# Two transformer blocks with eight experts: experts sorted by token count, three of them with a stacked high and low left operand

## The reference

```python
def moe_swiglu(h, w_router, w_gate, w_up, w_down):
    logits = jnp.einsum('bsd,de->bse', h.astype(F32), w_router.astype(F32))
    top_val, top_idx = lax.top_k(logits, TOP_K_EXPERTS)          # 2 of 8
    top_w = jax.nn.softmax(top_val, axis=-1)
    combine = jnp.sum(jax.nn.one_hot(top_idx, N_EXPERTS, dtype=F32) * top_w[..., None], axis=-2)
    for e in range(N_EXPERTS):
        out = out + combine[..., e:e + 1] * swiglu(h, w_gate[e], w_up[e], w_down[e])   # 1024 -> 2816 -> 1024
```

## Time and profile before

| | |
|---|---|
| median of 3 runs | 1914.62 us (1911.88 to 1915.4) |
| profiled execution, span | 1912.1 us |
| TensorE busy | 1824.1 us, 95% |
| VectorE busy | 1416.6 us, 74% |
| ScalarE busy | 1122.6 us, 59% |
| GpSimd busy | 392.8 us, 21% |
| mean granted TensorE clock | 0.983 |
| DMA | 506.45 MB, mean 265 GB/s |

### The profile page before, as it was taken

One profiled execution on the slowest core, in us unless ns is written; L12 is line 12 of the kernel. 1 busy time (PEld: TensorE's weight loads), 2 busy tenths in 40 slices (PEclk: granted clock), 3 DMA queues, 4 the chain that ended last, 5 costly groups with the idle time before them and its releaser, 6 DMA issues.

```text
span 1912.1 us, 26024 instructions
## 1 busy us (share of the span) xinstructions
PE 1824.1 (95%) x8799; PEld 1486.2 (78%) x8799; DVE 1416.6 (74%) x1631; ACT 1122.6 (59%) x1296; POOL 392.8 (21%) x315
## 2 busy tenths in 40 slices
PE   7899999989999998899989879999999999999997
PEld 6678886868888786688878667888888888888885
DVE  5748874466976586644458758889888888888897
ACT  6745444564443464443345537777777777777775
POOL 3722203463212363200046500000000000000000
PEclk9999999999999999999999989999999999999999
DMA  8348884418987341455544258999999999999994
GB/s 271 111 161 327 343 342 147 149 54 323 344 347 275 91 152 45 154 195 179 192 154 142 69 187 334 386 376 386 380 384 376 383 383 381 380 374 381 381 387 167
DMA packets 237934, 506.45 MB, mean 265 GB/s; under 512 B 23304, under 2 KB 74720, under 8 KB 231712
## 3 DMA queue, kind: packets, MB, share of 16 engines
q1 hardware_dynamic: 225664, 492.91, 70.9%
q0 software_dynamic: 3008, 10.32, 2.0%
q10 hardware_dynamic: 9184, 2.23, 0.5%
HBM read 497.49 MB, written 7.91 MB: 264 GB/s over the span
## 4 chain that ended last, share of the span: by engine, by line
PE 83%; DVE 7%; issue 6%; ACT 3%; POOL 1%; DMA 0%; POOLq 0%; SPq 0%; DVEq 0%; ACTq 0%
PE bank L2351 25%; PE bank L2353 25%; PE bank L2352 25%; PE bank L2470 2%; ACT slab L2042 1%; PE bank L2789 1%; DVE slab L1290 1%; PE bank L2561 1%; PE bank L2539 1%; ACT w_hi L1892 1%; PE bank L2521 1%; POOL w_lo L826 1%; DVE x L1074 0%; PE bank L2572 0%; DVE slab L1271 0%
## 5 line engine op out<-in xcount | busy, mean ns | idle before, releaser
L977 DVE TENSOR_TENSOR w_lo<-slab,w_hi 128x2048 fp32r<-128x2048 f32 x369 | 847.8, 2308 | 214.3 <-ACT w_hi L1892 213.3
L1892 ACT ACTIVATE w_hi<-slab 128x2048 fp32r<-128x2048 f32 (+2 forms) x421 | 796.6, 1898 | 329.0 <-PE bank L2353 256.3
L2351 PE MATMUL bank<-w_hi,hT_hi 128*128 128x512 f32 (+3 forms) x1664 | 649.4, 390 | 14.2 <-DVE hT_lo L1012 4.4
L2352 PE MATMUL bank<-w_lo,hT_hi 128*128 128x512 f32 (+3 forms) x1664 | 638.0, 383 | 0.0
L2353 PE MATMUL bank<-w_hi,hT_lo 128*128 128x512 f32 (+3 forms) x1664 | 637.9, 383 | 0.0
L2351 PEld LDWEIGHTS bank<-w_hi,hT_hi 128*128 128x128 f32 x1664 | 316.0, 190 | 77.9 <-DVE w_lo L977 8.8
L2353 PEld LDWEIGHTS bank<-w_hi,hT_lo 128*128 128x128 f32 x1664 | 315.5, 190 | 59.7
L2352 PEld LDWEIGHTS bank<-w_lo,hT_hi 128*128 128x128 f32 x1664 | 316.3, 190 | 55.3
L826 POOL TENSOR_TENSOR w_lo<-slab,w_hi 128x512 fp32r<-128x512 f32 (+2 forms) x208 | 262.4, 1295 | 381.3 <-ACT w_hi L1892 361.6
L2351 PE MATMUL bank<-w_hi,hid_hi 128*128 128x512 f32 x680 | 265.6, 391 | 0.7 <-DVE w_lo L977 0.7
L2353 PE MATMUL bank<-w_hi,hid_lo 128*128 128x512 f32 x680 | 265.0, 390 | 0.0
(11 more groups left out here) (252 smaller groups left out, 1232.0 us busy)
## 6 DMA issues: line engine op xcount, KB each, us to landing
slab<-in_w_exp_gate SPq DMA_DIRECT2D x176, 512.0 KB, 7.0
slab<-in_w_exp_up SPq DMA_DIRECT2D x176, 512.0 KB, 7.5
slab<-in_w_exp_down SPq DMA_DIRECT2D x176, 512.0 KB, 7.1
slab<-in_w_ada SPq DMA_DIRECT2D x48, 1024.0 KB, 5.5
slab<-in_w_mlp_in SPq DMA_DIRECT2D x64, 512.0 KB, 5.4
slab<-in_w_mlp_out SPq DMA_DIRECT2D x64, 512.0 KB, 9.0
slab<-in_w_in SPq DMA_DIRECT2D x56, 512.0 KB, 5.0
slab<-in_w_out SPq DMA_DIRECT2D x32, 512.0 KB, 4.6
```

The costliest lines, as they stand in the source:

```text
L977: dve.tensor_tensor(w_lo[:, q, 0:n], raw(s)[:, 0:n], w_hi[:, q, 0:n].bitcast(F32), ALU.subtract).then_inc(lo_dve, 1)
L1892: act.activation(w_hi[:, q, 0:n], raw(s)[:, 0:n], ACT.Copy).then_inc(hi_done, 1)
L2351: pe.matmul(dst, a_hi, b_hi, start=start, stop=False)
L2352: pe.matmul(dst, a_hi, b_lo, start=False, stop=False)
```

## The change

The inner columns of an expert are cut into three blocks of 768, 1024 and 1024 (`E_WIDTH`), each accumulated in two banks for gate and two for up. Weight tiles of gate and up hold two k blocks of a whole inner block, so a row of them is 3 or 4 KB long in HBM, where it was 2 KB (1 KB for the step of 256). An expert has 36 tiles (`MT`), eight of 1536 and two of 1024 columns among them, where it had 33. The sequence of a body is up, gate, the down tiles of the block before, turn. Down tiles of the last block run in the next body, with all three products.

The experts but number 0 are sorted on VectorE by the number of their tokens (`sort`, inside the first body): the four with the most take bodies 1, 3, 5 and 7, the others 2, 4 and 6 (`order`, read by SyncE for the addresses). In bodies 2, 4 and 6 the list has 64 places (`SHORT`). Its stationary operand is 128 columns wide all the same: columns 0 to 63 are the high parts, 64 to 127 the low parts, so that two products, with `w_hi` and with `w_lo`, give what three gave, plus low x low; the two halves of the result are added later: ScalarE moves rows 64 to 127 to rows 0 to 63 of SBUF, VectorE adds them, for gate and up. The output keeps both halves, and GpSimd adds them to `y_rows` by two scatters in turn. A second round follows if a list in a short body has more than 64, or another more than 128 entries. The residuals of all tiles are written by VectorE in one operation each.

The core of the diff:

```diff
-F_WIDE = 512
+
+E_WIDTH = (768, 1024, 1024)
+E_FROM = (0, 768, 1792)
+MS = len(E_WIDTH)
+MT = 36
+SHORT = P // 2
+SHORT_AT = (2, 4, 6)
+ROUND_SUMS = 16 * (3 + 4 + 2 * 3)
 ...
+        def is_short(p, first):
+
+            return p == 0 and not first
 ...
+        def up_tile(j, first):
+
+            return (0 if first else -4, 8, 20)[j]
+
+        def gate_tile(j, first):
+
+            return (4 if first else 0, 12, 24)[j]
+
+        def down_tile(j):
+
+            return (4, 16, 28, MT - 4)[j + 1]
+
+        def tile_width(r, first, last):
+
+            if r in (18, 19):
+                return D
+            return 2 * E_WIDTH[0] if r < 4 or first and r < 8 or r >= MT - 4 and not last else TILE
 ...
+                        def wide_rows(w, j, n, r0):
+
+                            for b in range(4):
+                                to, loaded = slot_free(n, r0 + b)
+                                d = to[:, 0:2 * E_WIDTH[j]].rearrange("p (k n) -> p k n", k=2)
+                                for k in range(2):
+                                    sp.dma_start(d[:, k:k + 1, :], w[:, 2 * b + k:2 * b + k + 1, E_FROM[j]:E_FROM[j] + E_WIDTH[j]]
+                                                 ).then_inc(loaded, 16)
 ...
+                            if n == n0 + 1:
+                                sp.wait_ge(order_done, 1)
+                            wg, wu, wd = weights(0 if first else sp.value_load(order[0:1, n - n0:n - n0 + 1], min_val=0, max_val=NE - 1))
+                            wide_rows(wu, 0, n, up_tile(0, first))
 ...
+                for a, o in enumerate((slice(0, SHORT), slice(SHORT, P)) if at in SHORT_AT else (slice(0, P),)):
+                    pool.wait_ge(scattered, done - (16 if at not in SHORT_AT else 32) + 16 * a)
+                    pool.indirect_dma_start(y_rows, bass.IndirectOffsetOnAxis(index[n % 2][0:o.stop - o.start, 0:1], 0), y_out[o, :], None,
+                                            compute_op=ALU.add).then_inc(scattered, 16)
 ...
+                    mark(dve.tensor_copy(rank_at[:, 0:1], iota[:, 0:1]))
+                    mark(dve.tensor_copy(rank_at[:, 1:NE:2], iota[:, 1:1 + NE // 2]))
+                    mark(dve.tensor_copy(rank_at[:, 2:NE:2], iota[:, 1 + NE // 2:NE]))
+                    mark(dve.memset(spare, 0.0))
+                    mark(dve.tensor_copy(counts[:, 1:NE], tot[:, 0, 1:NE]))
+                    link(dve.memset(counts[:, 0:1], 2.0 * SEQ))
+                    link(dve.memset(spare[:, 2:NE:2], float(P - SHORT)))
+                    mark(dve.tensor_tensor(at, across(counts), down_(counts), ALU.is_gt))
+                    link(dve.tensor_tensor(same, across(counts), down_(counts), ALU.is_equal))
 ...
+                    for src, to in ((wts, ranked_wts), (pos, ranked_pos)):
+                        link(dve.tensor_tensor(picked, each, src.unsqueeze(2).broadcast_to([P, TT, NE, NE]), ALU.mult))
+                        link(dve.tensor_reduce(to, picked, AX.X, ALU.add))
+                    link(dve.tensor_tensor(same, at, across(iota[:, 0:NE]), ALU.mult))
+                    link(dve.tensor_reduce(turns, same, AX.X, ALU.add))
+                    dve.tensor_copy(order[:, :], turns[0:1, :]).then_inc(order_done, 1)
 ...
+                    link(dve.tensor_tensor(counts, counts, spare, ALU.add))
+                    link(dve.tensor_reduce(den[0:1, 0, 0:1], counts[0:1, :], AX.X, ALU.max))
+                    dve.tensor_copy(flag[0:1, 0:1], den[0:1, 0, 0:1]).then_inc(flag_done, 1)
 ...
+                        def activated(j):
+
+                            at = ub + n * (2 * MS) + 2 * j
+                            banks = (bank[6], bank[7]) if first and j == 1 else (bank[4], bank[5])
+                            w = half_of(j)
+                            if short:
+                                base = half_base(turn_, i, j)
+                                for c, o in enumerate(halves(j)):
+                                    dve.wait_ge(half_moved, base + c + 1)
+                                    dve.tensor_tensor(mact[0:SHORT, o], bank[c][0:SHORT, 0:w], mact[0:SHORT, o], ALU.add
+                                                      ).then_inc(half_added, 1)
+                                for c, o in enumerate(halves(j)):
+                                    dve.wait_ge(half_moved, base + c + 3)
+                                    dve.tensor_tensor(up_low[:, o], banks[c][0:SHORT, 0:w], up_low[:, o], ALU.add
+                                                      ).then_inc(half_added, 1)
+                                for c, o in enumerate(halves(j)):
+                                    dve.wait_ge(act_done, at + c + 1)
+                                    dve.wait_ge(half_added, base + c + 3)
+                                    dve.tensor_tensor(mact2[0:SHORT, o], mact[0:SHORT, o], up_low[:, o], ALU.mult).then_inc(sq_done, 1)
+                            else:
+                                for c, o in enumerate(halves(j)):
+                                    dve.wait_ge(act_done, at + c + 1)
+                                    dve.tensor_tensor(mact2[:, o], mact[:, o], banks[c][:, 0:w], ALU.mult).then_inc(sq_done, 1)
 ...
+                        lows(2 if first else -2, gate_tile(0, first) + 6)
+                        activated(0)
+                        if first:
+                            lows(10, 14)
+                        else:
+                            lows(6, 10)
+                        hidden_low(0)
+                        if short:
+                            dve.wait_ge(w_used, FREE_SPLIT + EXPERT0 + n * MT + 8)
+                            dve.tensor_scalar(hid_lo[:, :, :], ones[:, 0:1].unsqueeze(2).broadcast_to([P, 4, SEQ]), 0.0, None, ALU.mult
+                                              ).then_inc(hid_zero, 1)
+                        if first:
+                            dve.nop().then_inc(hid_zero, 1)
+                        if first and n0 == 0:
+                            sort()
+                        if not last:
+                            lists(ranked_pos, ranked_wts, SHORT if p == 1 else P, 2 * i + p + 1, n + 1)
+                        lows(14 if first else 10, 18)
+                        activated(1)
 ...
+                            make_index(1 - p, n + 1, bank[6], None if first else sums_after(turn_, i, 0) if p else sums_after(turn_, i, 0) - 32)
+                            lows(22, 30)
 ...
+                            listed_rows(1 - p, n + 1, p == 1)
+                            lows(30, 34)
+                            hidden_low(2)
 ...
+                                    base = half_base(turn_, i, j)
+                                    for c, o in enumerate(halves(j)):
+                                        act.activation(mact[0:SHORT, o], bank[c][SHORT:P, 0:w], ACT.Copy).then_inc(half_moved, 1)
+                                    for c, o in enumerate(halves(j)):
+                                        act.activation(up_low[:, o], banks[c][SHORT:P, 0:w], ACT.Copy).then_inc(half_moved, 1)
+                                    for c, o in enumerate(halves(j)):
+                                        act.wait_ge(half_added, base + c + 1)
+                                        act.activation(mact[0:SHORT, o], mact[0:SHORT, o], ACT.Silu).then_inc(act_done, 1)
 ...
+                        def both(dst, hi_, lo_, q, s, start, stop_):
+
+                            if lo_ is None:
+                                pe.matmul(dst, hi_, w_hi[:, q, s], start=start, stop=False)
+                                return pe.matmul(dst, hi_, w_lo[:, q, s], start=False, stop=stop_)
+                            return product(dst, hi_, lo_, w_hi[:, q, s], w_lo[:, q, s], start, stop_)
+
+                        def rows_by(dst, j, r0):
+
+                            w = half_of(j)
+                            for b in range(4):
+                                q = low_ready(r0 + b)
+                                for k in (2 * b, 2 * b + 1):
+                                    l_hi, l_lo = lhs_listed(k + KC * p, 0)
+                                    for c in range(2):
+                                        s = slice((k % 2 * 2 + c) * w, (k % 2 * 2 + c + 1) * w)
+                                        ins = both(dst[c][:, 0:w], l_hi, None if short else l_lo, q, s, k == 0, k == KC - 1)
+                                ins.then_inc(w_used, 1)
 ...
+                        inner(0)
+                        gate(0)
+                        if first:
+                            inner(1)
+                            pe.wait_ge(ix_made, 2 * n + 2)
+                            turn(0)
+                        else:
+                            if p == 1:
+                                pe.wait_ge(hid_zero, i + (1 + (len(SHORT_AT) + 1) * turn_))
+                            sums(-1, False)
+                            turn(0)
+                            inner(1)
+                        gate(1)
```

(19 more changed lines are left out.)

525 lines of the change are left out of this document (304 added, 221 removed).

## The result

The changed kernel takes 1942.22 us (median of 4 runs, 1941.34 to 1946.76), the one before 1913.25 beside it: ratio 1.0159, 95% interval 1.0142 to 1.0176. It is slower by 29 us; the forecast was 1918.5, in a range of 1900 to 1934.

A forecast was written before the change was run, and what follows sets the result against it. TensorE was taken to bound the kernel before, VectorE the short experts after. Whole experts +11.6 and three short ones -7.7 gave +3.9 us on a span of 1912.1: 1916.0, median 1918.5, range 1900 to 1934.

The forecast's parts named there:

- Sorting, one round, TensorE's work: Expert stage: three experts short, no second round, about 180 products fewer; TensorE +0.3 us per whole expert, about 67.5 per short.
- VectorE is the bound of a short expert at 90.4 us: Short bodies: VectorE's summed work, 90.4 us, ends last, so 23 of TensorE's 26 us saved are not gained.
- I take 1.0 us idle in all: Short bodies: VectorE's idle time from handshake and slot waits, 1.0 us per short expert.
- -1.2 for the lead: Entry to a short body: VectorE is ahead of TensorE by 1.2 us, won back once.
- The longer rows take nothing off the end: Weight loads: 35.65 MB at 0.405 take 88 us per expert, under 91 and 95, so no gain by themselves.
- Rival 2: Short bodies: the stream of weights ends last, 92.6 to 95 us each; sum +7 to +18, 1926 us; chance 0.12.
- Whole experts, +1.5: Each whole expert: 1.2 us of waits from paired operations plus 0.3, between 0.3 and 4.
- the 0.3 of the narrow products: Whole expert on TensorE: 96 products of 384 columns make 90.5 us against 90.3, +0.3.
- First expert, +6.1 and last, +1.0: First body: sort stall 4.5, half clock 1.3, start -1.0, usual 1.0 + 0.3; last body: folding stalls, +1.0.
- Clock, 1.0 us per short expert: Short bodies: TensorE's half clock after its gaps behind each gate costs 1.0 us, between 0 and 5.
- Rival 3: Short bodies: TensorE's half clock stays, 3 to 4 us more per short body; 1929 us; chance 0.09.
- Rival 1: Expert stage: double buffers smooth the waits, VectorE idle under 1 us per short body; sum -10.0, 1904.6 us; chance 0.28.

The follow-up runs named there:

- the mended kernel: Changed kernel with down rows to all 128 partitions, the sort early, four split slots and the hidden rows one tile later: 1915.82 us, ratio 1.0022.
- the best kernel: The changed kernel with all four edits (full rows, early sort, four slots, later hidden rows), VectorE idle 2.6 to 4.0 us in short bodies: 1915.82 us.

## Why the prediction was wrong

The direction was right, though the forecast of +3.9 us lay on the line of what can be told and gave "slower" a chance of 0.43 only. The size was wrong by 23.7 us. Step by step:

- *Sorting, one round, TensorE's work*: right. 180 products fewer were forecast and 180 are gone; whole bodies have a floor of 94.0 us. (The text names 300 products of 512 columns for a whole expert; they are 324, as its sum has them.)
- *VectorE is the bound of a short expert at 90.4 us*: right as a sum, 1 to 2 us too high (88.6 to 89.5 seen). As a bound it was wrong for the changed kernel, where 6 us of its work less took off 2.7, and right in the main once the rest is mended: there 19 us of work in three bodies are worth 12.5 in the median.
- *"I take 1.0 us idle in all"*: this step failed. It was 8.4 to 8.8 us where the sum, with -1.2 for the lead and +1.0 for the clock, had 0.8; bodies took 97.6 on average where 91.2 was forecast: 19 of the 23.7 us. I followed one handshake, from the last gate tile, and took the other places by their sums. The runs showed three parts: the slots (2.0 to 4.2 us a body, by the run with three slots back), the places of the hidden rows in VectorE's queue (2 to 4 us a body, with four slots), and the loads to 64 partitions (2.9). All three are read against a profile of the mended kernel's fastest run, and so are rather too large. They sum to 9 us where the bodies got shorter by 5.8 in all: the causes overlap, and taking one away lets the next wait last, as the waits with four slots alone show. What is left, 2.6 to 4.0 us idle in a short body, has no run that takes it apart.
- *"The longer rows take nothing off the end"*: 4 KB rows do run at 408 to 417 GB/s, as the row of before said. But the step priced all bytes by that row, and 1 MB per expert goes to half the partitions: 257 GB/s over 8 us. The two lines stood in the diff, with the slice `o` on the partitions. Rival 2 (1926 us, short bodies held by the stream of weights) had one of the three causes, and a wrong reason for it (a mixed rate by row length). By the Trainium skill, SBUF — State Buffer, section "Door 1: The DMA port swizzle", partitions 0 to 63 reach eight of the 16 ports, and by its section "Can I just issue two DMAs to hit both halves?" a second transfer to the other half adds only 6%. The trace agrees, with 257 GB/s behind these loads against 379 behind the same bytes to all partitions; the prediction had not weighed that rule.
- *Whole experts, +1.5*: half right. Measured +2.6 on average. Four slots take 1.5 of it off, near the 1.2 that I had stepped out, and the later hidden rows 0.8, which I had not; the rest is the 0.3 of the narrow products.
- *First expert, +6.1 and last, +1.0*: measured +8.8 together. The stall of 4.5 and half clock of 1.3 were a gap of 4.04 and some 1.6.
- *Clock, 1.0 us per short expert*: right in size as far as one profile tells (0.9 with the gaps filled). Rival 3 is out.
- *Rival 1, VectorE at its floor*: the condition, idle under 1 us, was never met; the best kernel has 2.6. So no run had VectorE at its floor.

When one part alone is left unmended, the ratio stands above 1.0022 by 0.0044 for the loads to 64 partitions (8.4 us), 0.0064 for three slots (12 us) and 0.0045 for the early place of the hidden rows (8.6 us), each to some 0.003 (5 us), the last with four slots in both kernels. The sort was not put back alone; its share, 1 to 7 us, stays open between the profile and the medians.

## What to carry to other kernels

A bound worked out as one engine's sum is a floor. When engines with nearly equal sums (here 90.4 us and 88) pass work in a ring, step every place where an in-order queue can stand in front of a small operation, not the one that looks longest. Price a load by how many partitions it reaches as well as by its row length. When an edit gives nothing alone, look at which wait took its place before dropping it: here the fourth slot took 0.3 us off a short body alone, and cost 3.2 when it was taken away from the mended kernel. And before a gain is put down to one of two edits, compare the intervals: 0 and 9.4 us in the medians were the same 1.5 us in bodies 3 and 5.

## What was not expected of the hardware

- Four transfers of 256 KB, each to 64 partitions by 4 KB rows, in alternating halves: 257 GB/s over the 8 us behind them with the engines' share at 1.05, where 128 partitions by 2 KB rows gave 379, and 4 KB rows to all partitions 408 to 417. The share doesn't tell a slow stream from a full one.
- The granted clock of the short bodies was 0.91 to 0.95 without a loss that filling the gaps could win back in the median.
